# First quarter of a feed-forward's down projection: eight plain half products per unit in place of seven combined ones

## The reference, cut to what matters

```python
def conv_ffn(h, prev, w_up, conv_w, conv_b, w_down):
    u = h @ w_up                                   # 1024 -> 5632
    ext = jnp.concatenate([prev, u], axis=1)
    y = conv_b + sum(conv_w[k] * ext[:, k:k + l] for k in range(3))
    a, v = jnp.split(y, 2, axis=-1)
    return (jax.nn.silu(a) * v) @ w_down           # 2816 -> 1024
```

## Time and profile before

| | |
|---|---|
| median of 3 runs | 2927.24 us (2924.36 to 2935.34) |
| profiled execution, its own time | 2927.7 us |
| its span | 2925.9 us |
| mean granted TensorE clock | 0.972 |
| PE busy | 2742.8 us (94%), 20912 instructions |
| DVE busy | 1887.1 us (64%) |
| ACT busy | 1227.7 us (42%) |
| POOL busy | 1198.6 us (41%) |
| DMA | 272.87 MB, mean 93 GB/s |

### The profile page before, as it was taken

How to read it: one execution, slowest core, us unless ns; L and a number is a source line. 1 busy time by engine, 2 the same in 40 slices (tenths; PEclk the granted TensorE clock), 3 DMA queues, 4 the chain that set the end, 5 groups by cost and what they waited for, 6 DMA issues and landing times. The chain is left out here.

```text
span 2925.9 us, 54455 instructions
## 1 busy us (share of the span) xinstructions
PE 2742.8 (94%) x20912; PEld 2531.2 (87%) x20912; DVE 1887.1 (64%) x3412; ACT 1227.7 (42%) x2484; POOL 1198.6 (41%) x786
## 2 busy tenths in 40 slices
PE   8998979999999998999999799889998999998798
PEld 8998966666777898999999799888998999998798
DVE  6314048888555429778887666695358888878664
ACT  5001028888633325454545333315244545454332
POOL 3430000000000335555457777550436454557886
PEclk9999989999999999999999899999999999999999
DMA  6315750000467211222222222313112222232222
GB/s 190 103 51 175 252 182 16 2 2 2 156 202 226 100 45 44 85 71 86 71 85 96 95 90 75 136 36 120 44 43 67 71 85 71 86 113 92 96 83 88
DMA packets 168547, 272.87 MB, mean 93 GB/s; under 512 B 19936, under 2 KB 112454, under 8 KB 167110
## 3 DMA queue, kind: packets, MB, share of 16 engines
q1 hardware_dynamic: 139962, 224.20, 23.3%
q10 hardware_dynamic: 28332, 45.27, 4.7%
HBM read 226.84 MB, written 46.69 MB: 93 GB/s over the span
## 5 line engine op out<-in xcount | busy, mean ns | idle before, releaser
L3252 PE MATMUL banks<-token_blocks_high,weight_blocks_high 128*128 128x272 f32 x3584 | 754.1, 292 | 79.0 <-POOL weight_blocks_low L3139 46.0
L3252 PE MATMUL banks<-token_blocks_high,weight_blocks_low 128*128 128x272 f32 x3584 | 745.7, 290 | 0.0
L3252 PE MATMUL banks<-token_blocks_low,weight_blocks_high 128*128 128x272 f32 x3584 | 745.4, 290 | 0.0
L3252 PEld LDWEIGHTS banks<-token_blocks_high,weight_blocks_high 128*128 128x128 f32 x3584 | 567.0, 191 | 88.9 <-POOL weight_blocks_low L3139 52.0
L3252 PEld LDWEIGHTS banks<-token_blocks_low,weight_blocks_high 128*128 128x128 f32 x3584 | 569.5, 191 | 0.0
L3252 PEld LDWEIGHTS banks<-token_blocks_high,weight_blocks_low 128*128 128x128 f32 x3584 | 567.1, 191 | 0.0
L3139 POOL TENSOR_TENSOR weight_blocks_low<-ight_quarters_more,weight_blocks_high 128x512 fp32r<-128x512 f32 (+2 forms) x150 | 210.9, 1409 | 183.6 <-ACT weight_blocks_high L3276 181.7
L3534 DVE SCALAR_TENSOR_TENSOR conv_space<-conv_space,conv_w 128x1024 f32<-128x1024 f32 x176 | 237.5, 1349 | 73.7 <-ACT conv_space L3331 62.3
L3139 POOL TENSOR_TENSOR weight_blocks_low<-weights_whole,weight_blocks_high 128x512 fp32r<-128x512 f32 (+2 forms) x146 | 209.3, 1437 | 145.8 <-ACT weight_blocks_high L3276 144.8
L3139 POOL TENSOR_TENSOR weight_blocks_low<-weights_again_whole,weight_blocks_high 128x512 fp32r<-128x512 f32 (+2 forms) x146 | 205.6, 1413 | 144.3 <-ACT weight_blocks_high L3276 140.5
L3572 DVE TENSOR_TENSOR x<-x,banks 128x544 f32<-128x544 f32 x224 | 160.4, 718 | 156.4 <-PE banks L3252 152.4
(11 more groups left out here) (521 smaller groups left out, 5462.0 us busy)
## 6 DMA issues: line engine op xcount, KB each, us to landing
gated_scratch<-conv_space ACTq DMA_DIRECT2D x44, 544.0 KB, 3.6
past_rows<-in_kv_pages SPq DMA_DIRECT2D x160, 128.0 KB, 2.3
ight_quarters_more<-in_w_up SPq DMA_DIRECT2D x56, 256.0 KB, 2.9
weights_whole<-in_w_up SPq DMA_DIRECT2D x56, 256.0 KB, 3.0
weights_again_whole<-in_w_up SPq DMA_DIRECT2D x56, 256.0 KB, 3.0
staged<-gated_scratch SPq DMA_DIRECT2D x16, 816.0 KB, 7.9
z<-in_kv_pages SPq DMA_DIRECT2D x96, 128.0 KB, 2.5
x<-in_cmp_pages ACTq DMA_DIRECT2D x75, 128.0 KB, 4.0
```

Of the source, the lines that this page charges most:

```text
L3252: last = pe.matmul(out[:, piece, :], a[:, at], b[:, kk, piece * HP:(piece + 1) * HP], start=first and kk == 0 and z == 0, stop=kk == n - 1 ...
```

## The change

In both layers the first part of the down half (4 units) is computed plainly. A unit is 4 steps `(q, j)`, `PLAIN = 4`, tile `j // 2` and input half `j % 2`; a step multiplies one raw weight quarter with two raw token quadrants, 36 matmuls, and the second step of a tile adds in PSUM to the first. No weight sums, no token sums, 4 token blocks and not 7; DVE adds to `x` after every second step, two adds of 128 x 544. All four token blocks are rounded beside the last up unit. The second part's quadrants are loaded from ACT's queue at steps 7 and 8, and SP's list is no longer held for them. The preparation of the second part is placed at steps 10 to 15 of 16 (before: 16 to 27 of 28).

In layer 0's front: the near bias is loaded when the key weights (the first half of the last hidden layer) have been read; ACT multiplies the sample keys with the gain and takes the two roots apart, prompt blocks first; the reciprocal and product of the sample keys move to the end of DVE's list in `prompt_attention`; POOL waits for the last hidden layer before it writes its tables. TensorE gets 26 transposes of the identity between the first scores and the first turns.

```diff
-GATED_ORDER = (3, 2, 6, 4), (3, 4, 6, 2)
-JOINT_PARTS = (0,)
+GATED_ORDER = (3, 4, 6, 2)
+JOINT_PARTS = ()
+PLAIN = 4
...
-            sp.wait_ge(hidden, B)
+            sp.wait_ge(key_weights_read, 1)
             load_near_bias(k, sp, near_loaded)
...
             pool.wait_ge(near_loaded, 16)
+            pool.wait_ge(hidden, B)
             pool.memset(k.block_bias, NEG)
...
-            dve.reciprocal(rms[:, :], rms[:, :])
+            dve.reciprocal(rms, rms)
...
-            dve.scalar_tensor_tensor(out=comp_k[:, 0:B, :], ...)
...
+            act.wait_ge(finished, B)
+            act.activation(gained_keys, kc[:, 0:B * NCS], ACT.Copy, scale=c["gains"][:, Z_KS:Z_KS + 1])
             act.wait_ge(summed, 1)
-            act.activation(rms[:, :], key_sums, ACT.Sqrt, ...)
+            for dst, cols in ((rms, key_cols(B)), (key_rms, slice(0, B * NCS))):
+                act.activation(dst, key_sums[:, cols], ACT.Sqrt, ...)
...
+            for _ in range(26):
+                pe.transpose(turned_bank(0)[:, 0:P], c["ident"][:, :], c["ident"][:, :])
             pe.wait_ge(ident_rounded, 1)
...
+            gained_keys, key_rms = kept_keys(mix)
+            dve.reciprocal(key_rms, key_rms)
+            dve.drain()
+            dve.tensor_tensor(comp_k[:, 0:B, :], gained_keys..., key_rms..., ALU.mult)
             dve.wait_ge(tails_loaded, 16 * 2 * L)
...
+            def plain_product(q, j):
+                n, tile, kk_half = width(q), j // 2, j % 2
+                wait_split(pe, q, j)
+                if q == FC and j == 0:
+                    wait_read(pe, LAST, "C11")
+                    wait_read(pe, LEAD, "C21")
+                elif q == FC and j == 2:
+                    wait_read(pe, LAST, "C12")
+                    wait_read(pe, LAST, "C21")
+                elif kk_half == 0:
+                    wait_plain_read(pe, q - 1, tile)
+                if q == FC and j < 2:
+                    pe.wait_ge(d_split, 2 * j + 2)
+                wh, wl = ring(q, j)
+                for half in range(2):
+                    high, low = down_block(0, 2 * kk_half + half)
+                    out = plain_bank(tile, half)
+                    for kk in range(n):
+                        at = slice(kk * P, (kk + 1) * P)
+                        for z, (a, b) in enumerate(((wh, high), (wh, low), (wl, high))):
+                            for piece in range(2):
+                                last = pe.matmul(out[:, piece, :], a[:, at], b[:, kk, piece * HP:(piece + 1) * HP],
+                                                 start=kk_half == 0 and kk == 0 and z == 0, stop=kk_half == 1 and kk == n - 1 and z == 2,
+                                                 skip_group_check=True)
+                last.then_inc(multiplied, 1)
...
+            def stage_second(cols):
+                act.wait_ge(gated_stored, 16 * FC)
+                for kk in range(2):
+                    act.dma_start(gated_quadrants(1)[2 * kk + cols], stored_gated(1, kk, cols)).then_inc(staged_loaded[2 * kk + cols], 16)
...
+                if q == LAST and j in (2, 3, 4, 5):
+                    round_gated(0, j - 2)
...
-                for i in range(PER * BLOCKS):
-                    if p == 0 and i == 0:
-                        round_gated(0, 2)
-                    round_weights(BLOCKS * (FC - 1 + p * PER) + i + RING)
-                    if p == 0 and 0 < i and i + 2 < BLOCKS:
-                        round_gated(0, i + 2)
-                    if p == 0 and i == 9:
+                for i in range(PER * (BLOCKS if p else PLAIN)):
+                    round_weights(BLOCKS * LAST + PER * blocks_before(p) + i + RING)
+                    if p == 0 and i == 3:
                         silu(LAST)
-                    if p == 0 and i == 12:
+                    if p == 0 and i == 6:
                         store(LAST)
+                    if p == 0 and i in (7, 8):
+                        stage_second(i - 7)
                     if p + 1 < len(PAIRS):
-                        for j, at in zip(DOWN_ORDER, (16, 17, 24, 25, 26, 27, 27) if p == 0 else (7, 9, 23, 23, 24, 26, 27)):
+                        for j, at in zip(DOWN_ORDER, (10, 11, 14, 14, 15, 15, 15) if p == 0 else (7, 9, 23, 23, 24, 26, 27)):
...
             def add(q, j):
+                if plain(q):
+                    if j % 2:
+                        wait_product(dve, q, j)
+                        for half in range(2):
+                            xv = in_two(x[:, 2 * ((q - FC) % PER) + j // 2, half * TH:(half + 1) * TH])
+                            dve.tensor_tensor(xv, xv, plain_bank(j // 2, half), ALU.add).then_inc(x_added, 1)
+                    return
...
-            for j in GATED_ORDER[0][0:3]:
-                gated_sum(0, j)
+            lower_gated(0, 2)
+            lower_gated(0, 3)
...
-                        early = (17, 18, 20, 21, 22) if p == 0 else (9, 11, 12, 14, 16)
-                        late = (24, 25, 26, 27) if p == 0 else (21, 23, 24, 25)
+                        early = (11, 12, 12, 13, 13) if p == 0 else (9, 11, 12, 14, 16)
+                        late = (14, 14, 15, 15) if p == 0 else (21, 23, 24, 25)
```

More of the change, by code:

```diff
@@ L944, in first_stage, with kept_keys @@
     w.finish_stage(NZ, ())
+def kept_keys(spare):
+    return tuple(spare[:, R + x, 0:B * NCS] for x in range(2))
 def front(k, z, zs, spare, comp_k, comp_v, w1, gates, rows_loaded):
@@ L971, in front @@
         kc = k.sb(ctx, "cmp_keys", [P, B * NCS + NCP])
-        sq, rms = (rows[0][:, 4 * x:4 * x + 4, :].rearrange("p a n -> p (a n)")[:, 0:B * NCS + NCP] for x in range(2))
+        sq = rows[0][:, 0:4, :].rearrange("p a n -> p (a n)")[:, 0:B * NCS + NCP]
+        rms = rows[0][:, 4, 0:NCP]
+        gained_keys, key_rms = kept_keys(spare)
         attention_loaded = k.sem(ctx, "attention_constants_loaded")
@@ L1082, in hidden_layer @@
                             spread_tile(todo.pop(0))
+                    if b == B - 1 and kv == 0:
+                        last.then_inc(key_weights_read, 1)
                 last.then_inc(hidden, 1)
@@ L2914, in feed_forward, with plain, blocks_before @@
         LEAD, FIRST_PRODUCTS, FIRST_BLOCKS = LAST - 1, 8, 4
-        PRODUCTS = FIRST_PRODUCTS + BLOCKS * (UNITS - 1)
         SUMMED_BY_POOL = {1: 0, LAST: 1}
         DOWN_LEADS = tuple(FC + PER * p for p in JOINT_PARTS)
+        def plain(q):
+            return FC <= q < FC + PER
+        def blocks_before(p):
+            return 0 if p == 0 else PLAIN + BLOCKS * (p - 1)
         def joint(q, order):
@@ L2926, in feed_forward @@
             elif q - 1 not in DOWN_LEADS:
-                SEQUENCE += [(q, j) for j in DOWN_ORDER]
+                SEQUENCE += [(q, j) for j in (range(PLAIN) if plain(q) else DOWN_ORDER)]
         PLACE = {b: n for n, b in enumerate(SEQUENCE)}
+        ADDED = dict(zip(SEQUENCE[BLOCKS * LAST:], itertools.accumulate(j % 2 * 2 if plain(q) else 1 for q, j in SEQUENCE[BLOCKS * LAST:])))
+        PRODUCTS = FIRST_PRODUCTS + len(SEQUENCE)
         def at_place(n):
@@ L2968, in feed_forward, with last_block @@
         LAST_BLOCK = (2, 5, 4, 6)
+        def last_block(q, piece):
+            return piece if plain(q) else LAST_BLOCK[piece]
         BLOCK_PIECE = (0, 1, 0, None, 2, 1, 3)
@@ L2990, in feed_forward @@
             if q == FC:
-                SETS[q], SETS[q + 1] = (b1, SETS[LEAD][0], SETS[LEAD][0]), (e1, a1, a1)
+                PLAIN_SETS = b1, SETS[LEAD][0], e1, a1
+            if plain(q):
+                SETS[q] = (None, None, PLAIN_SETS[3])
+            elif q == FC + PER:
+                SETS[q] = PLAIN_SETS[0:3]
             elif q in DOWN_LEADS:
@@ L3004, in bank, with plain_bank, wait_plain_read @@
             return k.ps[:, 2 * s:2 * s + 2, 0:HP]
+        def plain_bank(tile, half):
+            s = PLAIN_SETS[2 * tile + half]
+            return k.ps[:, 2 * s:2 * s + 2, 0:HP]
+        def wait_plain_read(eng, q, tile):
+            eng.wait_ge(x_added, ADDED[q, 2 * tile + 1])
         def in_two(ap):
@@ L3015, in wait_read @@
             elif q >= FC:
[L3016 removed]
+                eng.wait_ge(x_added, ADDED[q, ("V1", "C11", "V2", "V5", "C22", "C12", "C21").index(what)])
             elif what in ("V1", "V2", "V5", "C21"):
@@ L3073, in feed_forward, with stored_gated @@
         g_dram = k.gated_dram
+        def stored_gated(p, kk, cols):
+            n, at = PAIRS[p], starts[p]
+            return g_dram[at + kk * n:at + (kk + 1) * n, :, cols * TH:cols * TH + TH].rearrange("k p t -> p k t")
         @block.sync
@@ L3113, in _ @@
                     stage_first(1)
-                elif q == FC + 2:
-                    stage(1)
+                elif q == FC + PER + 2:
+                    sp.wait_ge(gated, FC)
                     sp.dma_start(k.outs["conv"][layer], tails[:]).then_inc(stored, 16)
@@ L3168, in _ @@
                     second_sums(LAST)
-                elif q >= FC and j == 0 and q - 1 not in DOWN_LEADS and q not in DOWN_LEADS:
```

(15 more changed lines are left out.)

97 lines of the change are left out of this document (48 added, 49 removed).

## The result

The changed kernel takes **2901.95 us** (median of 4 runs, 2896.28 to 2903.72), the kernel before 2931.29 (4 runs, 2924.36 to 2938.61): ratio 0.9903, 95% interval 0.988 to 0.9925. It is 29.3 us faster. The forecast was 38.1 us less and 2889; the range 2878 to 2906 held the time, the bounds of the forecast's own case, 2882 to 2897, did not. The profiled execution took 2903.72 us, its span is 2901.9.

What follows compares the result with a forecast made beforehand. In the first down part PE was taken to lose 26.5 and 27.1 us, to POOL's blocks and sums and SP's held list. Terms 31.6 + 0 + 4.5 + 2 = 38.1 us off 2927.7 gave 2889.6, median 2889; range 2878 to 2906.

Steps and rivals of the forecast that it cites:

- the forecast's own case: Whole kernel: the forecast's terms hold, 2889 us, bounds 2882 to 2897; chance 0.55.
- Matmuls added: First down part: four plain units have 576 matmuls, 71.7 us, 9.0 us more than now, all on the path.
- sums and blocks removed: First down part: POOL's 44 instructions become 16, one per 4.48 us, at most 2.61 us each, so POOL cannot bind.
- Start: First down part's start: waits for low parts of token blocks, 2 us with small change, ends 0.7 and 5.3.
- Loads: First down part: weight refills have about 27 us for at most 11.6; quadrants go from ACT's list, SP no longer held.
- Rival 2: First down part: loads late anyway, POOL idle 10.50 us as now, 7.6 us a layer, 2904; chance 0.05.
- Entry of the second part: Second down part's first unit: waits of 5 to 6 us against 4.9 and 6.8 now, counted 0.
- rival 1: Second down part's entry loss doubles, DVE needing 2.8 us per block for 2.24 of product: 11.7 us more, 2901; chance 0.22.
- Front: Layer 0's front end: earlier near bias and shorter DVE work together gain 4.5 us, ends 0.7 and 5; each alone nothing.
- Transposes: Attention's first turns, layer 0: 26 transposes fill PE's wait and raise the clock, 2 us gained, ends 4.5 gained, 3 lost.
- sign for right: Second down part's first unit: 20 to 23 us would show the forecast.
- sign for wrong: First unit after the first down part: over 28 us would show the forecast wrong.

Runs made afterwards that it cites:

- a held SP: Changed kernel with the second part's quadrants issued from SP's list behind the wait for the last stored channel, as before the change: 2901.48 us, ratio 0.9899.
- the adds moved: Changed kernel with DVE's low parts of token blocks 3 to 6 of the second down part each put behind an add of that part: 2896.6 us, ratio 0.9883.
- the early version: Changed kernel with the second down part's preparation up to two steps earlier on DVE and ACT: 2882.95 us, ratio 0.9834.
- the second trace: The changed kernel run once more, nothing altered: 2900.85 us, ratio 0.9902.
- the two halves: Changed kernel with the near bias loaded late again, 2908.83 us; new feed-forward with the front of before and only the near bias early, 2904.43 us.

## Why the prediction was right, and where it was not

- *Matmuls added, 9.0 us a layer; sums and blocks removed.* Right: 71.87 us, POOL's blocks from the third on at 1.01 to 1.03 us with some 3.46 idle between them, PE always busy at the full clock.
- *Start, 2 us.* Too much: one wait of 0.94 us, and it falls between the up half and the part. So the first part gained 35.2 us and not 31.6. With the two waits counted in it is 33.4; in the table they are in the rest, where the third part (1.8 us less) makes up for them.
- *Loads.* Right, and with more room than thought: weights in 4.7 us, and no cost from a held SP. Rival 2 is out for the plain part.
- *Entry of the second part, taken as 0 with ends of -2.5 and +5.9 a layer.* **This is the step that failed**: the part grew by 2.85 and 6.04 us, 8.9 together (6.5 and 9.9 against the other two traces of before). The working followed when each token block would be *ready*, and that part was right: it had blocks 2, 3 and 4 at 5.8, 9.3 and 11.3 us of the unit, and DVE's rows above have them at 6.2, 9.2 and 11.0. From that it came to three waits of 1.2 to 2 us. It left out that the unit's products also need a PSUM set back, that this is an add in the same list, and that the add stood behind two adds of the plain part and two low parts. The real wait is one of 7.03 us, and about 2.6 us of half clock come on top of it. The case named as rival 1 (11.7 us more, 2901) came nearest. That the whole came out at its 2901 is in part luck: the entry cost 8.9, the first part gave 3.6 back, and stages that the change does not touch differ by more than that from trace to trace. Of its mechanism, that DVE's jobs are closer together holds, in so far as they stood ahead of the add. The rate of 2.8 us for each product of 2.24 is not seen: PE waits once in the unit and not from product to product, in the changed kernel and with the adds moved.
- *The shared port as told by the Trainium skill ("SBUF — State Buffer", section "SBUF: two separate sides").* The trace agrees with its rule as far as durations go: the same POOL instruction takes 1.03 us in the plain part, where DVE adds from PSUM or rests, and 2.61 beside DVE's low parts and sums (the row of 2655.27 in the earlier trace rows lies beside a low part of 2655.00). By the rule alone the unit would have been bound by POOL; it was not, since in the early version POOL needs 13.89 of 15.72 us. (The prediction calls this its second case; in its list it is rival 1.)
- *Front, 4.5 us.* Right: 4.7 (the front itself is no shorter, so the first scores came at 409.24 and not before the 406.5 named as a sign; in the second trace they came at 406.20), and the joint working (each alone nothing) was shown by the two halves.
- *Transposes, 2 us.* The stall was filled and the clock rose (0.63 to 0.88), but the attention gained 0.6 us on the mean, less than its traces differ; 26 took 4.06 us here, between the 3.1 and 6.2 worked out. In five of the six other traces that have them they took 3.06 us, the estimate for full clock, and PE then waited 0.68 to 0.69 us more.
- *The range.* It held the time because it reached from one rival to another; the forecast's own case did not. The unit's 25.3 us also lie between its sign for right (20 to 23) and its sign for wrong (28).
- *The rest.* The forecast was summed from one execution of before, 2927.7 us, which had its sample attention 4 to 7 us shorter than the two later traces. The median of before in these runs was 2931.3.

Term by term: the first part 3.6 us better, the entry 8.9 worse, front and transposes 0.6 worse make 32 us out of the 38.1. The medians give 29.3. The 3 us left over are less than the front (151 to 156 us), the sample attention (181 to 191) and the two feed-forward parts of before (330 to 336) differ from trace to trace, and stay open.

## What to carry to other kernels

When a wait is estimated at a seam (where one stage passes into the next), follow all that a product needs, its output space as much as its inputs, through the one list of the engine that frees it. When a stage has become pure matmuls, look where the helper engines stand idle in it and move the next stage's preparation there: this was worth 18 us here, more than half of what the large change brought. And two chains that end together must be shortened together.

## What the runs showed that was not expected

The granted clock in the first 34 us of the sample attention took values from 0.70 to 0.95 over the traces (0.80 to 0.95 in three of the same kernel, before), with PE busy 32 to 33 of the 34 us in each. The highest goes with the shortest stage, 181.6 us, and the lowest with 190.4 and 191.2; at 0.85, the value of nine traces, the stage still takes anything from 185.8 to 191.4. One trace is not enough to book such a stage's time to an edit elsewhere.
